# A depthwise convolution in a long TensorE-bound kernel: taps by sixteen with a turn through DRAM

## What is computed

```python
def conformer_conv(h, w_in, b_in, w_dw, b_dw, ln_g, ln_b, w_out, b_out):
    a, g = jnp.split(h @ w_in + b_in, 2, axis=-1)
    u = a * jax.nn.sigmoid(g)
    u = lax.conv_general_dilated(          # depthwise: each channel by itself, 31 taps, causal
        u, w_dw[:, None, :], window_strides=(1,), padding=[(CONV_WIDTH - 1, 0)],
        dimension_numbers=('NWC', 'WIO', 'NWC'), feature_group_count=D_MODEL) + b_dw
    mu = jnp.mean(u, axis=-1, keepdims=True)
    var = jnp.mean(jnp.square(u - mu), axis=-1, keepdims=True)
    u = (u - mu) * lax.rsqrt(var + LN_EPS) * ln_g + ln_b
    return jax.nn.silu(u) @ w_out + b_out
```

## Time and profile before

| | |
|---|---|
| runs | 2128.94 us median of 3 (2127.26 to 2129.07) |
| profiled execution | 2128.82 us, its span 2127.0 us |
| TensorE busy | 2087.1 us, 98% |
| VectorE busy | 1595.9 us, 75% |
| ScalarE busy | 1230.7 us, 58% |
| GpSimd busy | 56.6 us, 3% |
| TensorE's mean granted clock | 0.996 of full |
| chain that ended last | PE 91%, DVE 5%, ACT 3% |

### The profile page before, as it was taken

How to read it: one execution, slowest core, us unless ns; L and a number is a source line. 1 busy time by engine, 2 the same in 40 slices (tenths; PEclk the granted TensorE clock), 3 DMA queues, 4 the chain that set the end, 5 groups by cost and what they waited for, 6 DMA issues and landing times.

```text
span 2127.0 us, 39569 instructions
## 1 busy us (share of the span) xinstructions
PE 2087.1 (98%) x13444; PEld 1861.0 (87%) x13444; DVE 1595.9 (75%) x2803; ACT 1230.7 (58%) x2161; POOL 56.6 (3%) x78
## 2 busy tenths in 40 slices
PE   8999999999999999999999999999999999999998
PEld 8987889999999988878888888978888888888887
DVE  8687666999999975565557777887777777777776
ACT  4765455665666754544546556546556555656555
POOL 0020010000000000020000100000000000000000
PEclk9999999999999999999999999999999999999999
DMA  6442354555444455565566765415554555444554
GB/s 224 159 157 90 120 188 149 185 180 176 150 142 144 148 180 196 189 197 195 191 194 203 238 222 192 149 50 183 191 189 161 194 189 190 164 144 154 189 189 146
DMA packets 101115, 366.41 MB, mean 172 GB/s; under 512 B 11505, under 2 KB 12145, under 8 KB 100529
## 3 DMA queue, kind: packets, MB, share of 16 engines
q1 hardware_dynamic: 97776, 352.59, 50.0%
q0 software_dynamic: 3264, 12.85, 1.6%
HBM read 363.29 MB, written 2.10 MB: 172 GB/s over the span
## 4 chain that ended last, share of the span: by engine, by line
PE 91%; DVE 5%; ACT 3%; issue 1%; DMA 0%; DVEq 0%; ACTq 0%
PE acc L1784 16%; PE wide L2191 9%; PE wide L2192 9%; PE wide L2193 9%; PE acc L1789 8%; PE acc L1761 8%; PE acc L1762 8%; PE acc L1763 8%; PE wide L2177 2%; PE acc L2264 2%; DVE wlo L975 2%; PE sums L2024 1%; PE wide L1912 1%; PE wide L1914 1%; PE wide L1913 1%
## 5 line engine op out<-in xcount | busy, mean ns | idle before, releaser
L980 DVE TENSOR_TENSOR wlo<-raw,whi 128x1024 fp32r<-128x1024 f32 x396 | 488.5, 1234 | 207.0 <-ACT whi L463 201.9
L463 ACT ACTIVATE whi<-raw 128x1024 fp32r<-128x1024 f32 x450 | 475.3, 1056 | 229.0 <-PE wide L2193 228.6
L1761 PE MATMUL acc<-parts,whi 128*128 128x256 f32 (+1 forms) x1600 | 462.4, 289 | 2.6 <-DVE arena L1654 1.1
L1762 PE MATMUL acc<-parts,whi 128*128 128x256 f32 (+1 forms) x1600 | 453.4, 283 | 0.0
L1763 PE MATMUL acc<-parts,wlo 128*128 128x256 f32 (+1 forms) x1600 | 453.0, 283 | 0.0
L975 DVE TENSOR_TENSOR wlo<-raw,whi 128x1024 fp32r<-128x1024 f32 x268 | 327.8, 1225 | 103.1 <-ACT whi L458 91.5
L1784 PE MATMUL acc<-parts,whi 128*128 128x512 f32 x1504 | 375.0, 391 | 0.4 <-DVE arena L1725 0.4
L2191 PE MATMUL wide<-whi,small 128*128 128x512 f32 x896 | 351.2, 392 | 3.3 <-DVE small L1522 3.3
L2192 PE MATMUL wide<-whi,small 128*128 128x512 f32 x896 | 350.4, 391 | 0.0
L2193 PE MATMUL wide<-wlo,small 128*128 128x512 f32 x896 | 349.2, 390 | 0.0
L1784 PEld LDWEIGHTS acc<-parts,whi 128*128 128x128 f32 x1504 | 275.5, 188 | 53.4 <-issue 0.5
(11 more groups left out here) (350 smaller groups left out, 2355.0 us busy)
## 6 DMA issues: line engine op xcount, KB each, us to landing
raw<-stream SPq DMA_DIRECT2D x664, 512.0 KB, 3.3
arena<-taps_in POOLq DMA_DIRECT2D x20, 256.0 KB, 3.8
arena<-rows_in POOLq DMA_DIRECT2D x7, 512.0 KB, 4.6
arena<-h_in SPq DMA_DIRECT2D x2, 544.0 KB, 4.4
res<-rgw SPq DMA_DIRECT2D x1, 1024.0 KB, 8.7
res<-tokens_in POOLq DMA_DIRECT2D x1, 1024.0 KB, 5.2
park<-res POOLq DMA_DIRECT2D x1, 1024.0 KB, 4.2
res<-park POOLq DMA_DIRECT2D x1, 1024.0 KB, 6.2
```

The costliest lines, as they stand in the source:

```text
L463: act.activation(whi[:, c % RING, :], raw[:, c % RING, :], ACT.Copy).then_inc(hi_done, 1)
L980: V.tensor_tensor(wlo[:, c % RING, :], raw[:, c % RING, :], whi[:, c % RING, :].bitcast(F32), ALU.subtract).then_inc(lo_done, 1)
L1761: mm(out_, whi[:, s, w], xh, start=first, stop=False, **kw)
L1762: mm(out_, whi[:, s, w], xl, start=False, stop=False, **kw)
```

## The change

The tiles are shared anew: 0 and 1 for VectorE, 2 to 6 for TensorE in a new form ("quads"), 7 for TensorE in the old one. In the new form the 128 rows of a product are 32 channels at 4 shifts (0 to 3 columns), and the 128 columns of its weight are the same 32 channels at 4 offsets (0, 4, 8 and 12 taps). One product covers 16 taps of 32 channels, and two cover all taps of a group; a tile has four groups. The product has 268 columns. The rows at four shifts are made by transfers: the tile is written to DRAM (`tiles_d`) and read back four times, each a column further (`shifted_in`). The four offsets of the result are aligned likewise: ScalarE copies the banks to SBUF (`stage_out`), they go to DRAM (`offsets_d`), and four transfers bring each group back with the offsets side by side (`offsets_in`). VectorE adds the four and the bias (`join`, three operations). All these transfers are issued by GpSimd, which waits for the landing of each write before it reads. The quad products stand in `lin` behind cin's chunks 8, 10, 12, 14 and 15, in the four banks of `wide`. The diagonals shrink to 7168 columns, 14 transfers. At the end of ffn1 4 of the 46 filler products take other operands.

```diff
-        DW_DVE, DW_PE = (0, 1, 2), (3, 4, 5, 6, 7)
+        DW_DVE, DW_QUADS = (0, 1), (2, 3, 4, 5, 6)
         U = SEQ + TAPS - 1
         OVER = 16
-        DIAG = arena[:, 16384:16384 + 10240].rearrange("p (n g m c) -> p n g m c", n=5, g=2, m=8)
+        QW, QN = 284, SEQ + 12
+        DIAG = arena[:, 16384:16384 + 5120].rearrange("p (n g m c) -> p n g m c", n=5, g=4, m=2)
+        DIAG7 = arena[:, 21504:21504 + 2048].rearrange("p (g m c) -> p g m c", g=2, m=8)
         parts_of = ar(XN, SEQ, 4)
 
-        def doubled(n, g):
-
-            at = 8448 + n * 2 * U if n < 4 else 11776
-            return arena[:, at + g * U:at + (g + 1) * U]
+        def doubled(g):
+
+            return arena[:, 11776 + g * U:11776 + (g + 1) * U]
+
+        def quads(k):
+
+            return ar(8448 + k % 2 * 4 * QW, QW, 4)
+
+        def staged(k):
+
+            return ar(23552 + k % 2 * 4 * QN, QN, 4)
+
+        def joined(k):
+
+            return ar(25728 + k % 2 * 4 * SEQ, SEQ, 4)
...
-        LN_ORDER = [("dw_joined", 2, 3), ("dw_joined", 4, 4), ("dw_joined", 6, 5), ("dw_dve", 1, 0),
-                    ("dw_joined", 8, 6), ("dw_dve", 2, 1), ("dw_dve", 3, 2), ("dw_joined", 10, 7)]
+        LN_ORDER = [("dw_joined", 1, 2), ("dw_joined", 2, 3), ("dw_joined", 3, 4), ("dw_joined", 4, 5),
+                    ("dw_dve", 1, 0), ("dw_dve", 2, 1), ("dw_joined", 6, 6), ("dw_joined", 7, 7)]
...
+            def stage_out(k):
+                if k >= 4:
+                    act.wait_ge(sem("offsets_out"), 16 * (k - 3))
+                for g in range(4):
+                    act.wait_ge(sem("dw_pe"), 4 * (k - 2) + g + 1)
+                    act.activation(staged(k)[:, g, :], wide[:, g, 0:QN], ACT.Copy).then_inc(sem("staged"), 1)
...
+                if k in (9, 11, 13, 15):
+                    stage_out((k - 5) // 2)
+                if k in (12, 14):
+                    square((k - 12) // 2)
...
+            def part(g):
+                act.wait_ge(sem("dw_pe"), 20 + g + 1)
+                act.activation(parts_of[0:64, g, :], conv_bank(g)[64:128, OVER:OVER + SEQ], ACT.Copy).then_inc(sem("dw_part"), 1)
+            double(0)
+            stage_out(6)
+            double(1)
...
+            def join(k):
+                x = joined(k)
+                dve.wait_ge(sem(f"joined{k % 2}"), k // 2 * 64)
+                V.scalar_tensor_tensor(out=UC[:, k, :], in0=x[:, 0, :], scalar=v_("b_dw", k), in1=x[:, 1, :],
+                                       op0=ALU.add, op1=ALU.add)
+                link(V.tensor_tensor(x[:, 2, :], x[:, 2, :], x[:, 3, :], ALU.add))
+                V.tensor_tensor(UC[:, k, :], UC[:, k, :], x[:, 2, :], ALU.add).then_inc(sem("dw_joined"), 1)
...
+                if k in (11, 13, 15):
+                    join((k - 7) // 2)
...
+                if 2 <= k <= 8:
+                    take_taps(2 * (k - 2), 2 * (k - 1))
+                if k >= 9:
+                    take_taps(14 + 5 * (k - 9), 14 + 5 * (k - 8))
+            take_taps(49, 55)
+            join(5)
+            take_taps(55, 62)
+            join7(0)
...
+            join(6)
+            join7(1)
...
-                for _ in range(46):
+                if B == 4:
+                    for _ in range(4):
+                        mm(sums[:, 0:P], hh[:, 0, 0:P], hl[:, 0, 0:P], start=True, stop=True)
+                for _ in range(42 if B == 4 else 46):
...
+                    if behind is not None and k in behind:
+                        quad_taps(behind[k])
...
-            lin("cin", "mixpre0", after_pair=2)
-
-            def taps(n):
-                pe.wait_ge(sem(f"taps{n}"), 16 * 4)
-                pe.wait_ge(sem("doubled"), 4 * n + 4)
-                for g in range(2):
-                    q = 2 * n + g
-                    if q < 3:
-                        pe.wait_ge(READ["cin"], EV["cin"] + (DT - 1 if q == 0 else DT))
-                    else:
-                        pe.wait_ge(sem("dw_joined"), q - 2)
-                    for m in range(8):
-                        ins = mm(conv_bank(q)[:, 0:SEQ + OVER], DIAG[:, n, g, m, :], doubled(n, g)[:, 2 * m:2 * m + SEQ + OVER],
-                                 start=m == 0, stop=m == 7)
+            def quad_taps(k):
+
+                pe.wait_ge(sem("taps"), 14 * 16)
+                pe.wait_ge(sem(f"quads{k % 2}"), k // 2 * 64)
+                for g in range(4):
+                    if k > 2:
+                        pe.wait_ge(sem("staged"), 4 * (k - 3) + g + 1)
+                    for m in range(2):
+                        ins = mm(wide[:, g, 0:QN], DIAG[:, k - 2, g, m, :], quads(k)[:, g, 16 * m:16 * m + QN],
+                                 start=m == 0, stop=m == 1)
                     ins.then_inc(sem("dw_pe"), 1)
+            lin("cin", "mixpre0", after_pair=2, behind={8: 2, 10: 3, 12: 4, 14: 5, 15: 6})
+
+            def taps7(g):
+                pe.wait_ge(READ["cin"], EV["cin"] + DT)
+                pe.wait_ge(sem("doubled"), 2 * g + 2)
+                for m in range(8):
+                    ins = mm(conv_bank(g)[:, 0:SEQ + OVER], DIAG7[:, g, m, :], doubled(g)[:, 2 * m:2 * m + SEQ + OVER],
+                             start=m == 0, stop=m == 7)
+                ins.then_inc(sem("dw_pe"), 1)
...
-            for n in range(5):
-                taps(n)
-                if 1 <= n <= 3:
-                    k = LN_ORDER[n - 1][2]
-                    pe.wait_ge(sem("csq"), n)
-                    ln_sums(UC[:, k, :], sq(SEQ)[:, k, :], n == 1, False)
-            pe.wait_ge(sem("ln_added"), 3)
+            for n in range(2):
+                pe.wait_ge(sem("csq"), n + 1)
+                ln_sums(UC[:, n + 2, :], sq(SEQ)[:, n + 2, :], n == 0, False)
+                taps7(n)
+            pe.wait_ge(sem("csq"), 3)
+            ln_sums(UC[:, 4, :], sq(SEQ)[:, 4, :], False, False)
+            pe.wait_ge(sem("ln_added"), 2)
             ln_sums(ln_x_sum, ln_sq_sum, False, False)
+            pe.wait_ge(sem("staged"), 20)
             turn_over(wide[:, 3, 0:P], 8)
+            pe.wait_ge(sem("csq"), 7)
+            ln_sums(UC[:, 6, :], sq(SEQ)[:, 6, :], False, False)
             pe.wait_ge(sem("csq"), DT)
...
+            def shifted_in(k):
+                pool.wait_ge(sem("conv_in"), k + 1)
+                pool.dma_start(tiles_d[k - 2], UP[:, k, :]).then_inc(sem("tile_out"), 16)
+                pool.wait_ge(sem("tile_out"), 16 * (k - 1))
+                if k >= 4:
+                    pool.wait_ge(sem("dw_pe"), 4 * (k - 3))
+                for s in range(4):
+                    by_group = bass.AP(tiles_d.tensor, (k - 2) * P * (U + 2) + s, [[U + 2, 32], [32 * (U + 2), 4], [1, QW]])
+                    pool.dma_start(quads(k)[32 * s:32 * s + 32, :, :], by_group).then_inc(sem(f"quads{k % 2}"), 16)
+
+            def offsets_in(k):
+                pool.wait_ge(sem("staged"), 4 * (k - 1))
+                pool.dma_start(offsets_d[k - 2], staged(k).rearrange("p g n -> p (g n)")).then_inc(sem("offsets_out"), 16)
+                pool.wait_ge(sem("offsets_out"), 16 * (k - 1))
+                if k >= 4:
+                    pool.wait_ge(sem("dw_joined"), k - 3)
+                for g in range(4):
+                    by_offset = bass.AP(offsets_d.tensor, (k - 2) * P * 4 * QN + g * QN,
+                                        [[4 * QN, 32], [32 * 4 * QN + 4, 4], [1, SEQ]])
+                    pool.dma_start(joined(k)[32 * g:32 * g + 32, :, :], by_offset).then_inc(sem(f"joined{k % 2}"), 16)
+            shifted_in(2)
+            shifted_in(3)
+            for k in (2, 3, 4):
+                offsets_in(k)
+                shifted_in(k + 2)
+            offsets_in(5)
+            offsets_in(6)
```

More of the change, by code:

```diff
@@ L1615, in _ @@
             ffn(0)
+            V.memset(UP[:, :, U:U + 2], 0.0)
             link(V.memset(UP[:, :, 0:TAPS - 1], 0.0))
@@ L1634, in tap, with join7, take_taps @@
                     ins.then_inc(sem("dw_dve"), 1)
[L1635 to L1641 removed]
+            def join(k):
[5 more added lines that the diff above has]
+                V.tensor_tensor(UC[:, k, :], UC[:, k, :], x[:, 2, :], ALU.add).then_inc(sem("dw_joined"), 1)
+            def join7(g):
+                dve.wait_ge(sem("dw_pe"), 20 + g + 1)
+                dve.wait_ge(sem("dw_part"), g + 1)
+                V.scalar_tensor_tensor(out=UC[64 * g:64 * g + 64, 7, :], in0=conv_bank(g)[0:64, 0:SEQ],
+                                       scalar=vec[0:64, VEC["b_dw2"] + g:VEC["b_dw2"] + g + 1], in1=parts_of[0:64, g, :],
+                                       op0=ALU.add, op1=ALU.add).then_inc(sem("dw_joined"), 1)
+            tap_order = [(0, s) for s in range(4)]
+            for s in range(TAPS):
+                tap_order += [(1, s)] + ([(0, s + 4)] if s + 4 < TAPS else [])
+            def take_taps(lo, hi):
+                for n in range(lo, min(hi, len(tap_order))):
+                    tap(*tap_order[n])
             for k in range(16):
@@ L1847, in turn_half, with lin @@
                     ins.then_inc(sem("turned"), 1)
```

(25 more changed lines are left out.)

94 lines of the change are left out of this document (28 added, 66 removed).

## The result

| | before | after |
|---|---|---|
| median of the runs | 2128.23 us (2127.13 to 2129.07, 5 runs) | 2138.54 us (2138.0 to 2140.7, 5 runs) |
| profiled execution, span | 2127.0 us | 2136.7 us |
| mean granted clock | 0.996 | 0.992 |

The ratio is 1.0052, 95% interval 1.0037 to 1.0067: slower by half a per cent. Forecast were 2121.5 us, with 2137 as the top of the range. The time lies above the range, at the price of rival D, 2138.

What follows compares the result with a forecast made beforehand. TensorE bounds nearly everywhere, with VectorE equally full in the taps stage; afterwards GpSimd's queue. Sums at 1405.1 against 1411.8 (-6.5) and the tail (-1.2) gave -7.7, 2121.1, rounded to 2121.5 us; range 2115 to 2137.

Steps and rivals of the forecast that it cites:

- rival D: GpSimd's queue: issues of 1.0 us bring waits over 2 us at tiles 4 and 5; +9, 2138 us; chance 0.23.
- the ceiling at 1398: End of the taps stage: if only TensorE's work set the time, last sums at 1398 against 1411.8, -14.
- VectorE's work: Convolution stretch: fewer tap operations and half joins, five new joins; net 9.5 us less for VectorE.
- rival E: VectorE gets later than GpSimd's queue, its joins over twice as dear; chance 0.02, inside C.
- the prediction's sign against its account of VectorE: Last join: if VectorE rather than a gather stands ahead of it, the account of VectorE's work is off.
- the issue: GpSimd's queue between 1340 and 1397: 50 issues of 0.54 us each.
- Its second condition: Landings of 3.8 us in each place put the sums at 1417, making the kernel slower than before.
- C: GpSimd's queue eats the gain: landings of 3.4, 4.6, 3.4 us, sums at 1414.4; +1.7, 2130.5 us; chance 0.17.
- the landings: GpSimd's transfers: 2.6 us for a tile out, 3.6 for offsets out, 2.6 from the last gather's issue.
- the three pairs: GpSimd's queue from 1352.0: offsets of 2, 3, 4 with tiles 4, 5, 6, 10.9 us each, until 1384.7.
- The tail: Behind the last sums: without the pause before 1409.42, products and spreads run at full clock and start earlier, -1.2.
- the charge of 1.7 us for a fall: TensorE's wait before tile 6's quads: 3.4 us at half clock, 1.7 us of work lost, charged once.

Runs made afterwards that it cites:

- e5: Changed kernel without the turn through DRAM (shifts of rows and offsets left out; products, copies and joins stay): 2115.43 us, 0.9937 of the kernel before.
- e7: Changed kernel with thirteen chunks of weights loaded as 64 KB instead of 512 KB: 2132.12 us, 1.0012 of the kernel before.
- e12: Changed kernel with thirteen weight chunks thinned to 64 KB, tiles written from SyncE's queue and offsets from ScalarE's: 2121.21 us, 0.9968 of the kernel before.
- e2: Changed kernel with offsets written to DRAM from ScalarE's queue instead of GpSimd's: 2132.84 us, 1.002 of the kernel before.
- e4: Changed kernel with tiles written from SyncE's queue and offsets from ScalarE's, GpSimd issuing only gathers: 2132.3 us, 1.0015 of the kernel before.
- e8: Changed kernel with four tiles by quads at later chunks, tiles 6 and 7 in the old form, offsets from ScalarE's queue: 2126.4 us, 0.9993 of the kernel before.
- e10: Four-tile version (offsets from ScalarE's queue) plus 40 unread filler products ahead of tile 4's quads: 2127.32 us, 0.9994 of the kernel before.
- e6: Changed kernel with each gather fetching the same bytes as 32 rows of 4 KB instead of 128 short rows: 2142.09 us, 1.0062 of the kernel before.

## Why the prediction was wrong

**Right: what bounds the stage, and the work.** Quads at 0.46 a product (0.47 in e5), the ceiling at 1398 (e5: 1399.3), and VectorE's work, forecast at -9.5 us, measured at -11.2. Three of the five joins waited 4.7 to 6.0 us for their gathers, so rival E falls. The last join, at 1414.65, followed a split of weights without a wait, at about the time when its data were there (last gather issued at 1411.8, landing 2.7 us later), so the prediction's sign against its account of VectorE is neither there nor clearly absent.

**Right: the issue.** 0.55 us, forecast 0.54. Rival D's cause, issues of 0.8 to 1.0, is out, though its signs (waits of over 2 us at tiles 4 and 5) came true. That the time is at its price, 2138, is luck, since that price was worked out for issues of 1.0 us. Its second condition, landings of 3.8 in each place, is nearest to what happened: medians of 3.8 for both writes, 3.1 and 2.8 for the gathers, single ones up to 8.9. The 1417 that the prediction gives for it doesn't follow from the terms shown there. Four tile writes, four offset writes and three last gathers lie on the chain, so 3.8 in each place adds 4.8, 0.8 and 3.6 to 1405.1 and gives 1414.3, within C; the same count gives C's own 1414.4 to 0.3.

**The failed step: the landings.** I took 2.6, 3.6 and 2.6 us and called the medians of the earlier trace rows, 3.8 and 4.6, the far end. From the writes' issue to the moment that GpSimd goes on, where I had 2.8 and 3.8 with the wake, tiles out took 3.8, 5.4, 2.8, 4.1 and 5.6 us, offsets out 3.3, 9.2, 4.6, 4.1 and 3.3, and tile 2's last gather landed after 5.53 in place of 2.6. The 3.6 us row that I leaned on the earlier trace rows was one transfer at the head of cin, a stage with the DMA engines at 0.49. The change itself moved that share, cin's in the earlier trace rows, to 0.63, and that of the taps stage from 0.09 to 0.62: its ten transfers a tile, 1.76 MB (144 + 4 x 142 + 536 + 4 x 128 KB), lie beside the stream, and I used a share of before for a transfer of after.

The chain's own gathers are part of the load. The two writes of offsets that had no other transfer in flight, of tiles 2 and 6, landed after 3.0 us, less than my 3.6. Those of tiles 3, 4 and 5 were issued right behind four gathers and landed after 8.9, 4.3 and 3.8 (the GpSimd rows above show one of each kind). The one of 3.8 had no chunk of the stream in flight beside it. The one of 8.9 had two, and the first of them took 9.0 us itself. With the stream thin (e7) the two kinds still differ: 3.0 and 3.0, against 5.8, 4.5 and 3.9 behind gathers. No run tests the gathers' part by itself.

How far does this carry? Followed along the prediction's chain, with 3.41 us added to the times of after so that both stages start together, VectorE takes the sums up at 1423.8 and not at 1405.1, 18.7 us later:
- tile 2's write is issued 0.5 later; from there to its data takes 3.9 more;
- from these data to the write of its offsets takes 2.3 more, its quads at half clock;
- the three pairs take 42.6 us in place of 32.7, 9.9 more, of which the one landing of 8.9 us is 5.4;
- tile 6's data come 0.5 later still, its quads take 0.4 more, and from their end to the sums it is 1.2 more, the last sums at half clock.

So the landings carry 14.3 of the 18.7 us, and the clock most of the rest.

The Trainium skill, "DMA: Bandwidth & Descriptors" (Anatomy of one DMA), gives an estimate of 2.3, 3.3 and 2.3 us. Only the minima here, 2.5, 3.0 and 2.6, come near; beside the stream the rule gives no median. The same page (Queues, rings and completion order) says that each DMA engine takes turns between the queues it has work for, packet by packet. The trace agrees in direction: with the stream's bytes cut (e7) a tile out went from 3.8 to 2.6 in the median.

**Where the 19.9 us between -7.7 and +12.2 lie.** Waits ahead of quads 16.15 us in place of 5.7: 10.4. Quads 26.5 us in place of 20.0, four clock falls in place of one: 6.5. The last sums, 2.84 us where a like set took 1.68, again at half clock: 1.2. The tail, where the forecast -1.2 became +0.2: 1.4. Together 19.5. The last three are the clock's, 9.1 us, and the charge of 1.7 us for a fall was about right (1.9 for the sets of 5.54). What was wrong is the count. Three of the falls follow from the landings. The one at the last sums doesn't: I had tied it to the pause of 2.23 us and took 1.2 us off because that pause would go. The pause went, and the clock fell at this place all the same, here as in e5, with 0.45 us of idle ahead of the sums, and in e12. So this smaller term failed as well.

**The range.** It reached to 2137 since I ended it under D's worked out time. For a term whose ends lie far apart, more chance should have stood above: C's landings of 3.4 and 4.6 without further clock falls, and longer ones with them, were one continuous case.

**Open.** Two parts of the delay are shown, the stream (e7) and GpSimd's own queue (e2, e4), and e12 shows that they are distinct. The gathers' part is read from order in the traces alone. Which resource lengthens a single landing to 8 or 9 us (the queue that GpSimd's transfers go through, DRAM, the stream) no run tells apart.

## What to carry to other kernels

A chain of short transfers that wait for each other is priced by the landings at the load that the change itself makes, and by their spread, since TensorE meets the late one and not the median. Where a wait may pass 2 us, charge the half-clock stretch with it, and prefer a place with other products to run meanwhile: four tiles instead of five, with two tiles in the old form at the end, were worth 6 us here (e2 to e8, where fewer transfers, later places and the cover changed together). Before building such a turn, run the kernel without it (e5): it told in one run that 13 us were to be had and 23 were paid.

## What the runs showed of the hardware

A pause near 2.3 us may or may not cost the clock. Both executions stood for 2.27 us at the same place, near 527 us; before, 0.50 followed, after, the clock stayed at 1.00:

```profile
528.00:530.00 2.00, 2.00 (x19) 2.00 (x18) 2.00 (x4) 0.00 (x0) 1.41 (x1) 1.00 0.10 23
```

Near 1880 us it was the other way round, at the same wait of 2.40 us: the four records behind it took 0.92 us before (first row) and 1.65 after (second).

```profile
1873.78 0.92 PE L2082 MATMUL acc<-arena 128*128 128x128 f32 x4 [2.40 <-DVE arena L1318]
```

```profile
1882.52 1.65 PE L2111 MATMUL acc<-arena 128*128 128x128 f32 x4 [2.40 <-DVE arena L1334]
```

In e10 pauses of 2.45 and 2.62 us cost nothing either: the clock stayed at 1.00. Behind 2.27, 2.70, 5.00 and 6.18 us in the changed kernel it fell each time.

The clock also fell without a pause. After, TensorE was busy from 1400.54 on, from 1415.33 to 1420.32 mostly with one-column products (L2305), and from 1418 until past 1424 the clock was 0.50:

```profile
1418.00:1420.00 2.00, 2.00 (x11) 2.00 (x12) 0.00 (x0) 0.39 (x2) 0.00 (x0) 0.50 0.00 0
```

The same fall stands behind these products in e5 (from 1396 on) and e12 (from 1402 on), so the one in the kernel before, at 1412, need not be due to its pause.

And rows of 1 KB landed no later than rows of 4 KB (e6): gathers of 128 KB after 2.8 and 2.9 us in the median.
